# Feed-forward gate and up products: weight blocks as the stationary operand, 256 tokens moving

## The reference

```python
def rms_norm(x, g):
    y = x * lax.rsqrt(jnp.mean(x * x, axis=-1, keepdims=True) + 1e-6)
    return y * g

def swiglu_ffn(h, w_in, w_out):              # w_in: 1024 x 5632, w_out: 2816 x 1024
    gate, up = jnp.split(h @ w_in, 2, axis=-1)
    return (jax.nn.silu(gate) * up) @ w_out

x = x + 0.5 * swiglu_ffn(rms_norm(x, g), w_in, w_out)
```

## Time and profile before

| | |
|---|---|
| time, median of 3 runs | 1988.37 us |
| lowest, highest | 1986.28, 1990.23 us |
| the profiled execution: time | 1984.39 us |
| its span | 1982.6 us |
| mean granted TensorE clock | 0.988 |
| TensorE matmuls, weight loads busy | 1924.0 us, 1683.3 us |
| VectorE, ScalarE, GpSimd busy | 1378.4, 1090.6, 83.0 us |
| HBM read | 401.32 MB, 203 GB/s over the span |

### The profile page before, as it was taken

The page is one execution under the profiler, slowest core; times in us unless marked ns, Lnnn a source line. Parts: engine busy times, 40 slices in busy tenths (PEclk is TensorE's granted clock), DMA queues, the critical chain, the costliest instruction groups (busy, mean ns, idle before and its releaser), DMA issues. The chain is left out here.

```text
span 1982.6 us, 34175 instructions
## 1 busy us (share of the span) xinstructions
PE 1924.0 (97%) x14056; PEld 1683.3 (85%) x14056; DVE 1378.4 (70%) x1958; ACT 1090.6 (55%) x1639; POOL 83.0 (4%) x95
## 2 busy tenths in 40 slices
PE   7999998999999999999989999998999989999999
PEld 5888887999888888889889988887988988888888
DVE  5675875675666666666766666655876668999997
ACT  5444672554544544457455554444655447787785
POOL 1000006000000000000230000000000000000000
PEclk9999998999999999999999999998999989999999
DMA  9765430443665556544115366654333319999995
GB/s 391 275 232 191 141 115 24 148 163 138 244 253 205 208 200 250 211 168 151 65 52 199 138 224 231 234 191 115 128 128 128 139 60 354 374 374 376 370 372 201
DMA packets 56821, 404.54 MB, mean 204 GB/s; under 512 B 6424, under 2 KB 6608, under 8 KB 8416
## 3 DMA queue, kind: packets, MB, share of 16 engines
q1 hardware_dynamic: 51504, 370.73, 50.7%
q0 software_dynamic: 5168, 31.68, 4.5%
HBM read 401.32 MB, written 1.06 MB: 203 GB/s over the span
## 5 line engine op out<-in xcount | busy, mean ns | idle before, releaser
L306 DVE TENSOR_TENSOR weights_split<-ring,weights_split 128x1024 fp32r<-128x1024 f32 x696 | 819.8, 1222 | 207.8 <-ACT weights_split L296 203.4
L296 ACT CAST weights_split<-ring 128x1024 fp32r<-128x1024 f32 x696 | 693.5, 1048 | 213.5 <-PE ps L323 199.9
L321 PE MATMUL ps<-weights_split,act 128*128 128x512 f32 (+1 forms) x896 | 334.0, 373 | 12.8 <-DVE weights_split L306 12.7
L323 PE MATMUL ps<-weights_split,act 128*128 128x512 f32 (+1 forms) x896 | 329.1, 367 | 0.0
L322 PE MATMUL ps<-weights_split,act 128*128 128x512 f32 (+1 forms) x896 | 328.4, 367 | 0.0
L321 PEld LDWEIGHTS ps<-weights_split,act 128*128 128x128 f32 x896 | 168.8, 188 | 40.9 <-DVE weights_split L306 12.7
L323 PEld LDWEIGHTS ps<-weights_split,act 128*128 128x128 f32 x896 | 168.6, 188 | 28.5
L322 PEld LDWEIGHTS ps<-weights_split,act 128*128 128x128 f32 x896 | 168.9, 189 | 26.2
L321 PE MATMUL ps<-act,weights_split 128*128 128x256 f32 x608 | 175.9, 289 | 0.3
L322 PE MATMUL ps<-act,weights_split 128*128 128x256 f32 x608 | 171.5, 282 | 0.0
L323 PE MATMUL ps<-act,weights_split 128*128 128x256 f32 x608 | 171.3, 282 | 0.0
(11 more groups left out here) (544 smaller groups left out, 3369.0 us busy)
## 6 DMA issues: line engine op xcount, KB each, us to landing
ring<-stream SPq DMA_DIRECT2D x348, 1024.0 KB, 4.8
stretch<-ada_in POOLq DMA_DIRECT2D x24, 1024.0 KB, 5.2
y<-c_in POOLq DMA_DIRECT2D x4, 512.0 KB, 6.4
act_room<-mem_in SPq DMA_DIRECT2D x2, 1024.0 KB, 5.2
consts<-w_consts SPq DMA_DIRECT2D x1, 1376.0 KB, 11.6
x<-x_in SPq DMA_DIRECT2D x1, 1024.0 KB, 5.1
stretch<-mem_in POOLq DMA_DIRECT2D x1, 1024.0 KB, 9.6
bias_t<-bias_scratch POOLq DMA_DIRECT2D x1, 1024.0 KB, 13.2
```

The costliest lines, as they stand in the source:

```text
L296: core.nc.scalar.copy(self.hi[:, self.place(i), part], core.slot(chunk)[:, part]).then_inc(self.rounded.sem, 1)
L306: core.nc.vector.tensor_tensor(self.lo[:, self.place(i), part], core.slot(chunk)[:, part], self.hi[:, self.place(i), part].bitcast(F32), A ...
L321: nc.tensor.matmul(out, lhs[0], rhs[0], start=start, stop=False, **kw)
L323: return nc.tensor.matmul(out, lhs[1], rhs[0], start=False, stop=stop, **kw)
```

## The change

Weights become stationary in `gate_up`: for each of four blocks of 128 columns (two of gate, two of up) and four channel blocks, a weight block 128 x 128 is loaded and 256 tokens move. Gate goes to one bank, up to the next, with inner channels on the partitions. The transposes of hidden values (`turn_hidden`, `turn_last`) go. A token's norm factor now lies along the columns, so it is made as a row, the same on all partitions: a matmul with ones over the 256 sums, a root and a reciprocal of 128 x 256. VectorE multiplies the gate by it (`scale_gate`) ahead of Silu; up is left without the factor, and the sums of ten steps are multiplied by it where they are copied out of PSUM. In the last step both are scaled, in two halves of 128 inner columns each, and the down projection is done for the first half of the inner columns over all eight blocks, then (after the bias table's turning, in stage one) for the second. The feed-forward activations go from EVEN to ODD. The order of work on ScalarE and VectorE changes: round_hidden comes ahead of chunk 3j+4, multiply between the halves of chunk 3j+3.

```diff
-    def inner_bank(j, t):
-        return ps[:, (2 * j + t + 2) % 3, :]
+    def inner_bank(j, which):
+        return ps[:, (2 * j + which + 2) % 3, :].rearrange("p (m t) -> p m t", m=2)
+
+    def gate_or_up(j, m):
+
+        return inner_bank(j, m % 2)[:, m // 2, :] if j == steps - 1 else inner_bank(j, m // 2)[:, m % 2, :]
...
-            sg = stretch[:, 4096:5120].rearrange("p (a t n) -> p a t n", a=2, t=TT)
-            prod = stretch[:, 5120:5632].rearrange("p (t n) -> p t n", t=TT)
+            sg = stretch[:, 4096:5120].rearrange("p (a f t) -> p a f t", a=2, f=2)
+            prod = stretch[:, 5120:5632].rearrange("p (f t) -> p f t", f=2)
...
+        rs_row = core.sb("norm_row", [P, S], ctx=ctx)
+        both = rs_row[:, :].unsqueeze(1).to_broadcast([P, 2, S])
...
-                for t in range(TT):
-                    if half == 0 and 2 * j + t >= 3:
-                        pe.wait_ge(product.sem, product.at(2 * j + t - 2))
-                    if (j, half, t) == (0, 0, 1) and key[0] == "ffn2":
+                for m in (0, 2, 1, 3) if j == steps - 1 else range(4):
+                    which, opens = (m % 2, m < 2) if j == steps - 1 else (m // 2, m % 2 == 0)
+                    if half == 0 and opens and which == 0 and j >= 2:
+                        pe.wait_ge(product.sem, product.at(j - 1))
+                    if half == 0 and opens and which == 1 and j >= 1:
+                        pe.wait_ge(scaled.sem, scaled.at(j))
+                    if (j, half, m) == (0, 0, 2) and key[0] == "ffn2":
                         acts.await_made(pe, 6)
                     for k in range(4):
                         ch = 4 * half + k
-                        if j == 0 and t == 0:
+                        if j == 0 and m == 0:
                             acts.await_block(pe, ch)
-                        ins = products(nc, inner_bank(j, t), acts.parts(ch, slice(t * P, (t + 1) * P)),
-                                       [v[:, k, :] for v in w], ch == 0, ch == KB - 1)
-                    if (j, half, t) == (steps - 1, 1, 0):
-                        ins.then_inc(first_rows.sem, 1)
+                        ins = products(nc, gate_or_up(j, m), [v[:, k, m * P:(m + 1) * P] for v in w], acts.parts(ch),
+                                       opens and ch == 0, ch == KB - 1, skip_group_check=True)
+                    if (j, half, m) == (steps - 1, 1, 2):
+                        ins.then_inc(first_half.sem, 1)
                 ins.then_inc(core.used, 1)
...
-                pe.wait_ge(hidden.sem, hidden.at(j + TT))
                 w = weights.parts(i, "p (f n) -> p f n", f=2)
+
+                def add(o, f):
+                    return products(nc, ps[:, 3 + o // 2, (o % 2) * S:(o % 2 + 1) * S],
+                                    [v[:, f, o * P:(o + 1) * P] for v in w],
+                                    [v[:, j % 2, f, :] for v in (hid_hi, hid_lo)],
+                                    False, f == 1, skip_group_check=True)
+
+                pe.wait_ge(hidden.sem, hidden.at(j + 1))
+                for o in BLOCK_ORDER:
+                    add(o, 0)
+                if table:
+                    pe.wait_ge(product.sem, product.at(steps + 1))
+                    table.tensor_turn(pe, table_banks)
+                pe.wait_ge(hidden.sem, hidden.at(j + 2))
                 for place, o in enumerate(BLOCK_ORDER):
                     if o % 2:
                         pe.wait_ge(x_final.sem, x_final.at(place - 3))
...
+                    ins = add(o, 1)
...
-            acts.total(pe, 7)
+            acts.total(pe, 7, 6)
             for j in range(steps - 2):
                 gate_up(j + 1, 0)
-                turn_hidden(j)
                 gate_up(j + 1, 1)
...
+                down_proj(j, (0, 1))
             down_proj(steps - 2, (0, 1))
             if table:
                 table.tensor_sum(pe, spare_bank)
             gate_up(steps - 1, 0)
             gate_up(steps - 1, 1)
-            turn_last(0)
             turn_sums()
-            turn_last(1)
-            if table:
-                table.tensor_turn(pe, table_banks)
             last_down_proj()
...
             def silu_of(j):
...
+                act.wait_ge(scaled.sem, scaled.at(j + 1))
+                nc.scalar.activation(sg[:, j % 2], sg[:, j % 2], ACT.Silu).then_inc(silu.sem, 1)
 
             def round_hidden(j):
-                act.wait_ge(hidden_turned.sem, hidden_turned.at(j + 1))
+                act.wait_ge(product.sem, product.at(j + 1))
                 if j >= 2:
                     act.wait_ge(core.used, used_by(chunks(j - 2)[2]))
...
+                nc.scalar.copy(hid_hi[:, j % 2, :, :], prod).then_inc(hidden_rounded.sem, 1)
...
-            acts.root(act, 7)
+            acts.root(act, 7, rs_row, 6)
             act.wait_ge(acts.inverted.sem, acts.inverted.at(1))
             for j in range(steps):
                 if table and j == 5:
                     table.scalar_squares(act, acts.added)
                 elif table and j == steps - 1:
                     table.scalar_root(act, spare_bank)
-                silu_of(j)
+                if j < steps - 1:
+                    silu_of(j)
                 if j < steps - 2:
                     weights.round(act, 3 * j + 3)
+                    round_hidden(j)
...
+                    silu_last(0)
+                    silu_last(1)
+                    round_last(0)
+                    round_last(1)
...
+            def scale_gate(j):
+                dve.wait_ge(core.used, used_by(chunks(j)[1]))
+                nc.vector.tensor_tensor(sg[:, j % 2], inner_bank(j, 0), both, ALU.mult).then_inc(scaled.sem, 1)
+
             def multiply(j):
...
+                dve.wait_ge(silu.sem, silu.at(j + 1))
+                if j >= 1:
+                    dve.wait_ge(hidden_rounded.sem, hidden_rounded.at(j))
+                nc.vector.tensor_tensor(prod, inner_bank(j, 1), sg[:, j % 2], ALU.mult).then_inc(product.sem, 1)
...
+            def multiply_last(f):
+                j = steps - 1
+                dve.wait_ge(silu.sem, silu.at(j + f + 1))
+                if f == 0:
+                    dve.wait_ge(hidden_rounded.sem, hidden_rounded.at(j))
+                core.vchain(nc.vector.tensor_tensor(prod[:, f], sg[:, j % 2, f], rs_row[:, :], ALU.mult))
+                nc.vector.tensor_tensor(prod[:, f], gate_or_up(j, 2 + f), prod[:, f], ALU.mult).then_inc(product.sem, 1)
...
-                multiply(j)
+                if j < steps - 1:
+                    scale_gate(j)
                 if j < steps - 2:
-                    weights.subtract(dve, 3 * j + 3)
+                    weights.subtract_half(dve, 3 * j + 3, 0)
+                    multiply(j)
+                    weights.subtract_half(dve, 3 * j + 3, 1)
+                    subtract_hidden(j)
                     weights.subtract(dve, 3 * j + 4)
-                    subtract_hidden(j)
                     weights.subtract(dve, 3 * j + 5)
...
+                    for step in (scale_last, multiply_last, subtract_last):
+                        step(0)
+                        step(1)
...
+        if row_bank is not None:
+            self.core.nc.tensor.matmul(self.core.ps[:, row_bank, 0:S], self.core.const("ones"), self.sum[:, :], start=True,
+                                       stop=True)
...
+        if row is not None:
+            self.core.nc.scalar.activation(row[:, :], self.core.ps[:, row_bank, 0:S], ACT.Sqrt, bias=self.core.param("eps"),
+                                           scale=1.0 / D)
...
+            self.core.nc.vector.reciprocal(row[:, :], row[:, :])
...
-            mlp = normed("ffn1_norm_g", 0, "mlp", begun=0, phase=EVEN)
+            mlp = normed("ffn1_norm_g", 0, "mlp", begun=0)
```

More of the change, by code:

```diff
@@ L334, in ffn_stage @@
     start, _ = STREAM_AT[key]
[L335 to L340, removed]
+    scaled = core.sig("gate_scaled", steps + 1)
+    silu = core.sig("silu_ready", steps + 1)
+    product = core.sig("silu_times_up_ready", steps + 1)
+    first_half = core.sig("last_gate_up_first_half", 1)
+    hidden_rounded = core.sig("hidden_rounded", steps + 1)
+    hidden = core.sig("hidden_ready", steps + 1)
     sums_moved = core.sig("sums_in_sbuf", 2 * TT)
@@ L562, in _ @@
                 else:
-                    for t in range(TT):
-                        round_last(t)
+                    silu_last(0)
+                    silu_last(1)
+                    round_last(0)
+                    round_last(1)
             for i in range(1, further):
@@ L581, in subtract_hidden, with scale_last @@
             def subtract_hidden(j):
                 dve.wait_ge(hidden_rounded.sem, hidden_rounded.at(j + 1))
-                nc.vector.tensor_tensor(hid_lo[:, j % 2, :, :], turned, hid_hi[:, j % 2, :, :].bitcast(F32),
+                nc.vector.tensor_tensor(hid_lo[:, j % 2, :, :], prod, hid_hi[:, j % 2, :, :].bitcast(F32),
                                         ALU.subtract).then_inc(hidden.sem, 1)
```

(21 more changed lines are left out.)

92 lines of the change are left out of this document (28 added, 64 removed).

## The result

The changed kernel takes **2012.19 us** (median of four runs, 2010.46 to 2014.57) against 1987.32 for the kernel before, run beside it (1986.01 to 1990.23). The ratio is **1.0124** [1.0111, 1.0137]: slower by 24.9 us. The direction was forecast, the size was not: 2002 was said, and 2012.19 lies 1.2 us above the range. The profiled execution took 2010.46 us with a span of 2008.7, 26.1 us above the span of before, at a mean granted clock of 0.983 against 0.988.

A forecast was written before the change was run, and what follows sets the result against it. TensorE's issue was taken to bound the kernel. Terms 15.4 - 19.2 + 11.7 + 3.4 + 2.6 = +13.9 us gave 1998.3 on the profiled execution, 2002 us on the median's footing, range 1989 to 2011.

The forecast's parts named there:

- Bound now: Feed-forward stages: a step costs what TensorE issues, 16.80 us; other engines' work is free until a chain comes too late.
- A: Gate and up matmuls: 96 of 256 columns at 117 ns replace 48 of 512, +15.4 us over 44 steps.
- Rivals 2 to 5: Gate-up matmuls: exactly half, 1987 us (5%); faster, 1977 at 111 ns (9%); 121 ns, 2019 (7%); loads unhidden, 2300 (1%).
- B: Transposes of hidden values removed from TensorE's steps: 40 turns of 0.48 us, -19.2 us.
- C: Start of each of four stages: the longer norm-factor chain delays chunk 3 for TensorE, +11.7 us in all.
- my stall of 2.6 us: Each stage's start: TensorE idle ahead of the second half of gate-up 1, waiting for the chunk 3 split, 2.6 us.
- D: Last but one step: hidden values reach down projection 9 late by 0.85 us, four times, +3.4 us.
- E: Ends of stages: split last down projection and later bias table turning shift the adds into x, +2.6 us in sum.

The follow-up runs named there:

- the offset experiments: Changed kernel with feed-forward activations at EVEN (0 bytes) instead of ODD: 2025.23 us, ratio 1.0197; changed kernel with ODD as 64 bytes instead of 32: 2010.53 us, ratio 1.0127.
- The doubled turns: Kernel before, with each of the 160 transposes of turn_hidden done twice into the same place: 2005.67 us, ratio 1.0085.

## Why the prediction was right and wrong

- **Bound now**: right. TensorE's issue sets every step, before and after.
- **A**: right. 116.7 ns of the predicted 117; that 0.3 ns is 1.3 us. The choice of the nearest row by offset held, and the offset experiments show it is the offset that chooses. By the gap that the Trainium skill gives (TensorE: Matmul & The Clock Gate, Back-to-back issue gap) it would be, estimated, some +5 us; the trace has +14.1. Rivals 2 to 5 fall with the stretch rows.
- **B**: right, 0.455 a turn for 0.48. The doubled turns say 0.43 for four more. The step of 16.67 was met.
- **C**: wrong, and here the whole miss lies. The step that failed is the sentence "The table load, 1.28, now hides under the reciprocal". It ran at once in the earlier trace rows because the wait ahead of it there was already met. The change puts another wait ahead of Silu, for the scaled gate, and I moved the load as if it belonged to the root, and did not ask which waits stand before it. Price: 5.2 us. Worse, my stall of 2.6 us was held to cost 2.6. With the load it became a bank wait of 0.5 and an idle of 3.0 us, and TensorE's clock halved behind it in three of four stages: 5.7 us more. The rest of C, the chain's durations and overlaps in sum, was 11.5 for 11.7. The upper bound of +15 allowed for a longer Silu and no overlap, and for nothing of the clock.
- **D**: right, 0.89 for 0.85. TensorE waits ahead of down projection 9; these two matmuls start 1.00 us apart, where 0.23 is usual:

```profile
668.75 0.39 PE L323 MATMUL ps<-weights_split,mlp_hidden_lo 128*128 128x512 f32 x1
669.75 0.47 PE L321 MATMUL ps<-weights_split,mlp_hidden_hi 128*128 128x512 f32 x1 [0.60 <-DVE mlp_hidden_lo L572]
```

- **E**: right in sum, 1.7 for 2.6, within its bounds. VectorE's adds into x at the ends of stages two, one and four, and the turning of the bias table on TensorE, answering to the earlier trace rows:

```profile
692.70 0.78 DVE L648 SCALAR_TENSOR_TENSOR x<-ps,x 128x256 f32<-128x256 f32 x2 [0.20 <-PE ps L323]
...
214.15 0.74 DVE L648 SCALAR_TENSOR_TENSOR x<-ps,x 128x256 f32<-128x256 f32 x2
...
1368.70 2.94 DVE L648 SCALAR_TENSOR_TENSOR x<-ps,x 128x256 f32<-128x256 f32 x8 [3.09 <-PE ps L323]
```

```profile
207.45 3.79 PE L1823 MATMUL ps<-bias_t,consts 128*128 128x512 f32 x8
```

  Gate-up ends at 686.51, so the add comes at +6.2 (said: +6.3). In stage one gate-up ends at 201.82 and the turning begins at +5.63 (said: +5.65). In stage four x is whole at 1371.64, +9.1 from 1362.50 (said: 9.2). Stage one's end cost 2.3 (said 2.4) and stage four's -0.7 (said -0.6). Stages two and three were misjudged twice: their ends came 0.2 us sooner and not 0.3 later, and gate-up 0 of stage three took 0.8 longer and not 0.2; the two errors nearly cancel. These make 2.0; the ledger has 1.7 since it books A in full at each gate-up 0, which grew by 0.25 and not 0.32.
- **What was not in the sum**: gate-up 0 of stage one took 1.0 us more than its width explains. It seems to belong to the execution: in six other kernels with the change at this offset the same stretch took 0.24 to 0.99 us more than before, and in the two that leave it as it was before, 0.62 and 0.97. What follows stage four, which the change does not touch, was 4.05 us longer than in this one execution of before; the ten other kernels lay +2.4 to +5.0 there. This goes with the clock. After stage four the execution of before is at half clock for 35 us, the changed kernel's for 49, the others' for 42 to 52. So the execution of before was a lucky one in its last third, as its 1984.39 us beside a median of 1988 says too. It matters little to the result, since the ratio comes from medians and the stages alone make +24.5.

The chance of 0.76 for slower was of the right kind. The range failed by the clock: with the table load alone the time would have been some 2006.5, inside it. Had I let the 2.6 us of idle cost twice in its upper end, four times, it would have reached past 2012.

## What to carry to other kernels

Where a change adds or moves a wait near the first use of another activation function, ask which wait the table load will stand behind; a wait that is implied by another is not free. An idle of some 3 us on a TensorE at full clock cost 0.05 to 2.7 us on top through the clock, so its upper bound is nearly twice its length; short chains at a stage's start are best cured by doing the next transfer or split while the engines are idle ahead of it: here that took 19 of 25 us.

## What the runs showed of the hardware

- Filling the idle with 24 useless matmuls in each of four stages made the kernel 5.6 us faster, through the clock.
- The half clock behind the same idle is not the same in each stage: none in stage two, 3.4 us in stages one and four, 6.8 in stage three, at an idle of 3.0 to 3.1 us in each, after a shorter one of 0.5 (1.0 in stage one). Nor is it the same in the same stage: in the two offset runs, with idles alike, it was 6.8, 0, 3.4 and 3.4 us at 0 bytes and 3.4, 0, 0 and 3.4 us at 64.
- A moving operand of 256 columns costs by where it begins: activations beside stationary weights 120, 116.7 and 117.8 ns per matmul at 0, 32 and 64 bytes. For moving weights beside stationary activations, in the cross-attention, the best is another one. 192 of them at 32 bytes, in the changed kernel, and at 64:

```profile
396.15:418.84 22.69, 22.69 (x195) 22.69 (x194) 15.47 (x24) 11.98 (x19) 0.00 (x0) 1.00 0.48 181
```

```profile
397.20:418.95 21.75, 21.75 (x194) 21.75 (x193) 14.74 (x22) 12.00 (x20) 0.00 (x0) 1.00 0.51 188
```

  22.69 us against 21.75, 118.8 and 113.9 ns. Here 64 bytes win, and half of a matmul of 512 columns (113.3) is nearly met. No run joined the two, 32 bytes for the feed-forward's activations and 64 for these; by the rows it would be worth some 2 us.
- The inverse of 128 x 256 values takes VectorE 1.75 us, 2.5 times the 0.69 us of a product of 128 x 512.
